# Attention weights turned in half tiles of 64 rows, beside the scores

## The reference

```
for l in range(2):
    h = rms_norm(x, g_pre) @ w_in
    # selected blocks (slc), window 512 (win), compressed keys: 4 heads, head size 64
    # latent attention (mla): 4 heads, query and key size 96, value size 64
    # window 128 (swa): 8 heads, head size 64
    P = softmax(q @ k.T * scale + bias, masked to causal keys)
    o = P @ v
    x = x + rms_norm(concat(o) * silu(z) @ w_out, g_post)
```

## Time and profile before

| | |
|---|---|
| median of 3 runs | 1339.13 us (1339.0 to 1339.31) |
| span of the profiled execution | 1336.9 us |
| attention of layer 0 | about 840 to 975 us of the span |
| attention of layer 1 | about 1145 to 1281 us of the span |
| PE busy | 96% of the span |
| DVE, ACT, POOL busy | 52%, 31%, 30% |

### The profile page before, as it was taken

The page is one execution under the profiler, slowest core; times in us unless marked ns, Lnnn a source line. Parts: engine busy times, 40 slices in busy tenths (PEclk is TensorE's granted clock), DMA queues, the critical chain, the costliest instruction groups (busy, mean ns, idle before and its releaser), DMA issues.

```text
span 1336.9 us, 23888 instructions
## 1 busy us (share of the span) xinstructions
PE 1289.2 (96%) x9603; PEld 792.8 (59%) x9603; DVE 694.1 (52%) x1422; ACT 413.4 (31%) x898; POOL 395.5 (30%) x470
## 2 busy tenths in 40 slices
PE   5999999999999999999999999998999999998997
PEld 3454555655666677678445786445655786445653
DVE  4366667845333344464465373237736383337735
ACT  4243313362432222201014112236613202236721
POOL 0100001221324443153531240128731150127731
PEclk9999999999999999999999999999999999999999
DMA  9710112101410100032244415110003515100001
GB/s 318 267 63 28 37 64 79 63 0 64 142 51 3 65 2 3 2 126 72 94 177 100 129 32 189 64 52 1 2 16 76 147 38 189 63 1 2 1 1 63
DMA packets 71532, 96.54 MB, mean 72 GB/s; under 512 B 27639, under 2 KB 35247, under 8 KB 71422
## 3 DMA queue, kind: packets, MB, share of 16 engines
q1 hardware_dynamic: 71050, 94.76, 21.1%
q10 hardware_dynamic: 372, 0.27, 0.1%
HBM read 92.89 MB, written 2.13 MB: 71 GB/s over the span
## 4 chain that ended last, share of the span: by engine, by line
PE 84%; DVE 5%; SPq 3%; POOL 2%; ACT 2%; issue 1%; DMA 1%; POOLq 0%; DVEq 0%; ACTq 0%
PE PS L147 81%; PE PS L2791 2%; DVE AR L2897 1%; SPq L187 1%; POOL AR L3078 1%; POOL AR L2014 1%; DMA bias_rows<-AR 1%; ACT AR L3019 1%; DMA AR<-in_final_g 1%; SPq L308 1%; SPq L304 0%; SPq L309 0%; SPq L312 0%; POOL AR L3076 0%; DVE AR L2884 0%
## 5 line engine op out<-in xcount | busy, mean ns | idle before, releaser
L147 PE MATMUL PS<-AR 64*64 64x64 f32 (+14 forms) x8966 | 1217.3, 331 | 21.6 <-ACT AR L3029 6.3
L147 PEld LDWEIGHTS PS<-AR 128*128 128x128 f32 (+4 forms) x8966 | 723.4, 155 | 485.6 <-issue 387.0
L3019 ACT ACTIVATE AR<-AR 128x257 f32<-128x257 f32 (+5 forms) x160 | 84.9, 530 | 98.3 <-DVE AR L2897 88.7
L2897 DVE CUSTOM_DVE_ANT_0 AR<-PS,AR 128x257 f32<-128x257 f32 (+5 forms) x160 | 72.3, 452 | 60.7 <-PE PS L147 43.1
L412 POOL TENSOR_TENSOR AR<-AR 128x1 f32<-128x1 f32 (+4 forms) x26 | 21.9, 841 | 258.0 <-DVE AR L407 211.2
L1189 DVE SCALAR_TENSOR_TENSOR AR<-AR 128x441 f32<-128x441 f32 (+2 forms) x96 | 78.6, 819 | 15.7 <-ACT AR L1146 12.0
L1576 DVE TENSOR_TENSOR AR<-PS,AR 128x256 f32<-128x256 f32 x60 | 25.5, 425 | 100.7 <-PE PS L147 97.6
L3078 POOL TENSOR_SCALAR AR<-AR 128x257 f32<-128x257 f32 (+5 forms) x96 | 53.4, 556 | 58.8 <-DVE AR L2903 51.3
L3076 POOL TENSOR_SCALAR AR<-AR 128x128 f32<-128x128 f32 (+3 forms) x64 | 38.9, 608 | 63.3 <-DVE AR L2903 58.3
L1703 ACT ACTIVATE AR<-PS 128x512 f32<-128x512 f32 x48 | 28.7, 597 | 92.5 <-PE PS L147 90.0
L2014 POOL TENSOR_TENSOR AR<-AR 128x512 f32<-128x512 f32 x36 | 47.4, 1318 | 28.0 <-DMA AR<-in_w_o 24.9
(11 more groups left out here) (264 smaller groups left out, 941.6 us busy)
## 6 DMA issues: line engine op xcount, KB each, us to landing
AR<-in_w_in SPq DMA_DIRECT2D x16, 2048.0 KB, 8.9
AR<-in_w_mod SPq DMA_DIRECT2D x6, 2048.0 KB, 12.7
AR<-in_w_out SPq DMA_DIRECT2D x4, 2048.0 KB, 12.5
AR<-in_x SPq DMA_DIRECT2D x8, 512.0 KB, 5.2
AR<-in_w_in SPq DMA_DIRECT2D x4, 1024.0 KB, 7.3
AR<-in_w_o SPq DMA_DIRECT2D x2, 2048.0 KB, 7.7
AR<-in_w_in SPq DMA_DIRECT2D x2, 1664.0 KB, 8.6
AR<-in_w_in SPq DMA_DIRECT2D x12, 256.0 KB, 4.1
```

Source lines behind the costliest of these rows:

```text
L147: return t.matmul(o, l, r, start=s, stop=p, skip_group_check=True)
L2897: v.do.tensor_tensor_reduce(PB[j % NJP][e][:, 0:nk], ps["s", l, j, e][:, 0:nk], bias_for(qb, kind, 2 * a + e, nk), 1.0, 3e38, ALU.add, ALU ...
L3019: a_.do.activation(P, P, ACT.Exp, bias=mn[:, j % NJS, e:e + 1], scale=-1.0, accum_out=su[:, j % NJS, e:e + 1]).then_inc(sa, na("p", l, j, e))
```

## The change

Each 128x128 block of weights is transposed as two half tiles: 64 rows of queries in, 128 rows (keys) by 64 columns out. Rows 0 to 63 go to PSUM bank 3 and rows 64 to 127 to bank 4 of the pair, one after the other. Every job now takes both banks (`take_two`) before its first half tile, and the counter tells that it is turned once, after its last. A narrow job is still one copy, now over both banks; of a wide one DVE copies bank 3 and ACT bank 4, both with both heads' columns. The product reads its 128 columns as two runs of 64. Scores get four banks (0, 1, 2, 5) after the gates. On PE the turn is placed next to the score of its iteration. DVE's and ACT's own sequences stay.

```
-        few = itertools.cycle((0, 1)), itertools.cycle((3, 4))
-        all_ = itertools.cycle((2, 0, 1)), itertools.cycle((5, 3, 4))
+        few, all_ = itertools.cycle((0, 1)), itertools.cycle((0, 1, 2, 5))
...
         def turn(j):
+
             qb, kind, a = JOBS[j]
             k0, nb, nk, at = keys_of(qb, kind)
+            p = ps.take_two(t, "pT", l, j, bank=TURNED)
             for e in range(2):
                 t.wait_ge(sg, ng["normed", l, j, e])
-                if e == 0 or not narrow(j):
-                    p = ps.take(t, "pT", l, j, "both" if narrow(j) else e, bank=next(rings[1]))
-                c = 256 * e if narrow(j) else 0
                 for b in range(nb):
-                    x = t.go.transpose(p[:, c + 128 * b:c + 128 * b + 128], PB[j % NJP][e][:, at[b]:at[b] + 128], ident)
-                if e in halves(j):
-                    x.then_inc(st, nt("pT", l, j, e))
-            if narrow(j):
-                x.then_inc(st, nt("pT", l, j, "both"))
+                    for r in range(2):
+                        c = 512 * r + 64 * (nb * e + b)
+                        x = t.go.transpose(p[:, c:c + 64], PB[j % NJP][e][64 * r:64 * r + 64, at[b]:at[b] + 128],
+                                           ident[64 * r:64 * r + 64, 64 * r:64 * r + 64])
+            x.then_inc(st, nt("pT", l, j))
...
         for i in range(NJ + PV):
-            rings = few if i <= FILLED else all_
-            if i % 2 == 0:
-                turned(i), filled(i), scored(i), summed(i)
+            ring_ = few if i <= FILLED else all_
+            if i <= FILLED and i % 2 == 0:
+                filled(i), turned(i), scored(i), summed(i)
+            elif i <= FILLED:
+                summed(i), scored(i), turned(i), filled(i)
+            elif i % 2 == 0:
+                scored(i), turned(i), summed(i)
             else:
-                summed(i), scored(i), filled(i), turned(i)
+                summed(i), turned(i), scored(i)
...
-        e_.wait_ge(st, nt["pT", l, j, e])
+        e_.wait_ge(st, nt["pT", l, j])
         if j >= NJT:
             e_.wait_ge(st, nt["pv", l, j - NJT])
-        p = ps["pT", l, j, e]
...
         write(dst, src).then_inc(sem, count("pT", l, j, e))
-        ps.empty(sem, count, "pT", l, j, e)
+        ps.empty(sem, count, "pT", l, j)
```

More of the change, by code:

```diff
@@ L2705, in program @@
     TURN, PV = 4, 6
+    TURNED = 3
     CMP_EXP, CMP_SUM, CMP_TURN, CMP_PV = 1, 2, 5, {1: 0, 4: 1}
@@ L2764, in score @@
                 r = slice(64 * e, 64 * e + 64)
-                p = ps.take(t, "s", l, j, e, bank=next(rings[0]))
+                p = ps.take(t, "s", l, j, e, bank=next(ring_))
                 if kind == "mla":
@@ L2776, in score_cmp @@
         def score_cmp(qb):
-            p = ps.take(t, "scc", l, qb, bank=next(rings[0]))
+            p = ps.take(t, "scc", l, qb, bank=next(ring_))
             for a in range(2):
@@ L2784, in turn @@
             k0, nb, nk, at = keys_of(qb, kind)
+            p = ps.take_two(t, "pT", l, j, bank=TURNED)
             for e in range(2):
                 t.wait_ge(sg, ng["normed", l, j, e])
-                if e == 0 or not narrow(j):
-                    p = ps.take(t, "pT", l, j, "both" if narrow(j) else e, bank=next(rings[1]))
-                c = 256 * e if narrow(j) else 0
                 for b in range(nb):
-                    x = t.go.transpose(p[:, c + 128 * b:c + 128 * b + 128], PB[j % NJP][e][:, at[b]:at[b] + 128], ident)
-                if e in halves(j):
-                    x.then_inc(st, nt("pT", l, j, e))
-            if narrow(j):
-                x.then_inc(st, nt("pT", l, j, "both"))
+                    for r in range(2):
[3 more added lines that the diff above has]
+            x.then_inc(st, nt("pT", l, j))
         def turn_cmp(qb):
             t.wait_ge(sg, ng["pc", l, qb])
-            p = ps.take(t, "pcT", l, qb, bank=next(rings[0] if qb else rings[1]))
+            p = ps.take(t, "pcT", l, qb, bank=next(ring_) if qb else TURNED)
             t.go.transpose(p[:, 0:128], Pc.rearrange("p h c -> p (h c)"), ident).then_inc(st, nt("pcT", l, qb))
@@ L2817, in product @@
                         vv = VN_[:, k0 + b, v0:v0 + 64]
-                    x = mm(t.go, o[64 * e:64 * e + 64, c], vv, PT[j % NJT][:, e, 128 * b:128 * b + 128],
-                           b == 0 and kind != "win", b == nb - 1)
+                    x = mm(t.go, o[64 * e:64 * e + 64, c].rearrange("p (r x) -> p r x", r=2), vv,
+                           PT[j % NJT][:, :, 64 * (nb * e + b):64 * (nb * e + b) + 64], b == 0 and kind != "win", b == nb - 1)
             x.then_inc(st, nt("pv", l, j))
@@ L2875, in out_of_psum @@
         w_ = 128 * keys_of(qb, kind)[1]
-        e_.wait_ge(st, nt["pT", l, j, e])
+        e_.wait_ge(st, nt["pT", l, j])
         if j >= NJT:
             e_.wait_ge(st, nt["pv", l, j - NJT])
-        p = ps["pT", l, j, e]
[L2880 to L2883, removed]
+        src, dst = (x[:, :, 0:w_] if e == "both" else x[:, e, 0:w_]
+                    for x in (ps.two("pT", l, j).rearrange("p (r n) -> p r n", r=2), PT[j % NJT]))
         write(dst, src).then_inc(sem, count("pT", l, j, e))
-        ps.empty(sem, count, "pT", l, j, e)
+        ps.empty(sem, count, "pT", l, j)
     def attn_v(v, l):
@@ L2895, in least @@
                 if j >= NJP:
-                    v.wait_ge(st, nt["pT", l, j - NJP, "both" if narrow(j - NJP) else e])
+                    v.wait_ge(st, nt["pT", l, j - NJP])
                 v.do.tensor_tensor_reduce(PB[j % NJP][e][:, 0:nk], ps["s", l, j, e][:, 0:nk], bias_for(qb, kind, 2 * a + e, nk), 1.0, 3e38,
```

## The result

The changed kernel takes 1397.03 us (median of 4 runs, 1394.36 to 1399.03) against 1339.07 us: a ratio of 1.0432, with an interval of 1.0419 to 1.0444. It is slower by 58 us. The forecast was slower, by 16 us, with a range of 1344 to 1371 us; the time lies above it.

What follows compares the result with a forecast made beforehand. PE's order of work bounds the attention's last third, POOL the middle. 6.9 + 1.0 (DVE's lateness) + 1.9 - 1.5 - 0.2 = 8.1 us per layer, 16.2 for two: span 1353.1, median 1355.3 us, range 1344 to 1371.

Steps and rivals of the forecast that it cites:

- The chain: Attention, iterations 13 to 39: score, least, expo, copy, turn stand between two turns; 45.0 us, loop +6.9 per layer; chance 0.78.
- hand-over: Same loop: 13 hand-overs of an estimated 0.05 us behind the waits, 0.6 us per layer.
- Half tiles do overlap: PE's turns: strictly alternating row halves overlap fully, 0.062 us a block, 0.046 less than before.
- The rival of serial halves: PE's turns: half tiles do not overlap, a block costs 0.125 us, 8 us more per layer, 1371 us; chance 0.07.
- the 107 ns each: PE's weight loads: the skill's rule, two loads 213 ns a block, 20 us more in one layer's turns, iterations 13 to 39.
- The rival in which PE gets faster: Attention: both banks are free in time and PE sets the pace, 6.5 us less per layer, 1326 us; chance 0.09.
- the clock stays at 2.4 GHz in the new gaps: PE in the attention: a clock falling in the new gaps would prove the prediction wrong; it fell in no stretch shown.
- The gates' end: From the turns behind the gates to least of 13: 3.3 us in place of 4.8, so -1.5 us per layer.
- the early iterations: Iterations 4 to 11, while the gates run: gate matmuls cover ACT's copy and turns get cheaper, -0.2 us per layer.
- the compressed turns: In the loop of iterations 13 to 39: eight products or turns of compressed keys, 0.45 us each, 3.6 us per layer.
- the sum: From score 13 to score 39: chain, turns, products, compressed keys and hand-overs make 75.6 us per layer, before 68.6.
- The tail: From the score of 39 to the last product: 10.9 us in place of 9.0, so +1.9 us per layer.

Runs made afterwards that it cites:

- e1: Changed kernel with DVE and ACT copying out turned weights ahead of least and expo in every iteration: 1353.2 us, ratio 1.0106.
- e8: Kernel before, with only DVE and ACT copying out turned weights first in every iteration: 1340.5 us, ratio 1.0012.
- e2: Changed kernel with three score banks (0, 1, 2) after the gates in place of four: 1405.6 us, ratio 1.0495.
- e5: e2 plus matmuls whose results nobody reads, sized to each gap ahead of the even turn: 1386.5 us, ratio 1.0351.
- e6: Changed kernel with DVE copying out the turned compressed weights ahead of least in iterations 15, 25 and 35: 1394.4 us, ratio 1.041.
- e7: e1 plus DVE copying out the turned compressed weights ahead of least in iterations 15, 25 and 35: 1346.5 us, ratio 1.0048.
- e4: Kernel before (whole tiles, its own banks) with only PE's new order of steps: 1362.9 us, ratio 1.0176.
- e10: e4 with four score banks, and banks 3 and 4 taken in turn, one by a narrow job: 1362.2 us, ratio 1.018.
- e11: e7 with the compressed weights turned one iteration later, in iterations 6, 16, 26 and 36: 1334.07 us, ratio 0.9968.

## Why the prediction was right in direction and wrong in size

**The chain is what I said it was.** The timeline of iteration 33 after (start, length, instruction):

```profile
967.94 0.46 PE L2792 MATMUL PS<-AR 64*128 64x64 f32 x8
968.18 0.31 PEld L147 LDWEIGHTS PS<-AR 64*128 64x128 f32 x4
969.51 0.69 DVE L2897 CUSTOM_DVE_ANT_0 AR<-PS,AR 128x512 f32<-128x512 f32 x1
971.15 0.72 ACT L3019 ACTIVATE AR<-AR 128x512 f32<-128x512 f32 x1
972.05 0.60 ACT L3029 ACTIVATE AR<-PS 128x512 f32<-128x512 f32 x1
972.71 0.28 PE L2792 MATMUL PS<-AR 64*128 64x64 f32 x2 [2.53 <-ACT AR L3029]
```

The score is loaded at 968.18 and the copy ends at 972.65: 4.47 us, priced at 4.35. The turn of the even iteration follows 0.06 us later, a hand-over priced at 0.05. e1, which takes the copies out of the chain, takes back 44 us; e8 shows that the same edit is worth nothing where no turn waits for the pair of banks.

**Half tiles do overlap.** Eight of them in alternating halves, after:

```profile
914.12 0.46 PE L2792 MATMUL PS<-AR 64*128 64x64 f32 x8
```

Less 0.22 us for the last one, 0.24 us are seven steps: 0.034 us each, against 0.031 predicted. The rival of serial halves falls. So does, for loads that follow each other, the 107 ns each by the rule that the Trainium skill gives (TensorE: Matmul & The Clock Gate, LDWEIGHTS). The rival in which PE gets faster falls by the same waits that carry the chain.

**The step that failed: that the clock stays at 2.4 GHz in the new gaps.** I named its fall as what would make the prediction wrong, and took from the fact that it "did not in any stretch shown here" that it would stay at 1.00. But PE was busy 94 to 96% there, and the chain I had just forecast was to take that away. After, the two loops hold 37.5 and 41.0 us at half clock, and with the rest of the span there are some 98 us (2 x 1395.5 x 0.035), against 8 before. At the 0.29 us for each that e2 and e5 give, the 90 us more are an estimated 26 of the 58 us. The ratio is carried over from two other kernels; the four runs of this one bear it out over 14 us only, and at the 0.53 of e1's layers it would be 48. So it is shown that the clock is a part, and not how large a part.

**The gates' end and the early iterations: +3.2 us in place of -1.7 per layer.** The banks' rule costs there too. In iteration 5 the compressed turn takes bank 3 of the pair behind ACT's copy, which stands behind two exponentials:

```profile
862.02 0.38 ACT L3029 ACTIVATE AR<-PS 128x256 f32<-128x256 f32 x1
...
862.55 0.30 PE L2799 MATMUL PS<-AR 128*128 128x128 f32 x1 [1.81 <-ACT AR L3029]
```

PE is idle for 1.81 us, and the clock is at half for 3.4 us behind it. I had costed the compressed turns as PE's work only. The gain at the gates' end, forecast at 1.5 us, was about 0.4: from the turn behind the gates (897.96) to least of 13 (902.07) it is 4.1 us, with another turn ahead of the gates, in place of 4.8.

**The compressed turns in 15, 25 and 35: no term of the sum had their bank.** They take one of the four score banks, now ahead of the scores of two iterations, and in the second of these the second head's score waits for DVE's copy of them:

```profile
978.67 0.29 DVE L2925 COPY AR<-PS 128x128 f32<-128x128 f32 x1
979.01 2.08 PE L147 MATMUL PS<-AR 96*128 96x512 f32 x2 [1.75 <-DVE AR L2925]
```

From least of 35 to least of 37 the round took 10.25 us (10.9 between the loads of their scores), where the terms of the sum make 6.5. Some of that is clock: from 979 to 985 us, behind this wait, it was 0.50. By itself that wait is nearly covered by the chain (e6: 2.6 us), but it is worth 6.7 us when the chain is gone (e7).

**The tail: +3.7 us in place of +1.9.** The term was there, at half its size; part of it ran at 1.2 GHz (0.87 in the window 993 to 1006).

**The sum.** 16 us as forecast, some 26 for the clock by the estimate above, and some 16 for the early iterations, the compressed turns' banks and the tail, which I get only as the remainder. The range failed with it: its upper end was set by half tiles that don't overlap, and no case in it had the clock, though the text named it. A loss of clock that feeds on a forecast wait should have been one of the rivals, with the chain's own gaps as its condition.

What stays open is the order of PE on its own. I took it as harmless without the pair of banks. e4 and e10 show 23 to 24 us for it, with two different sets of banks, and waits of 9.6 and 2.9 us for ACT's copy in e10. Their mean clocks, 0.987 and 0.993, are some 35 and 19 us at half clock against 8 before. For e10 even 0.53 for each of the 11 us more is 6 of the 23 us, an estimate, so there the waiting is the larger part; no run separates the two.

## What to carry to other kernels

Ahead of making two steps share a buffer, follow who frees it: if the engine that copies it out does so behind work that needs a later step of the producer, a chain closes around the loop, and turning that engine's order round is worth more than the change itself (44 us here, in a kernel where the same reversal had been worth nothing). Whoever forecasts new gaps on TensorE must price what its clock does in them too. And a wait that hides inside a longer one shows its worth only when the longer one is gone (2.6 us, then 6.7 us for the same edit), so try such edits together and in this order.

## What the runs showed of the hardware

The granted clock fell to 1.2 GHz again and again though PE was busy 73 to 82% of the stretches and was never idle for more than 3.1 us at once; in e2, with gaps of 0.5 to 1.7 us ahead of the even turns and of up to 2.1 us ahead of scores, its mean was 0.79 over 98 us. In e11 it stayed at 1.00 in a window of layer 0 in which PE was busy 84% of the time, and was 0.93 from 1200 to 1278 us in layer 1: within one execution the same work kept the clock once and lost it once. Matmuls with no use, put only into the gaps, made a kernel 19.1 us faster (e5 against e2). Half tiles of 64 rows in alternating row halves followed each other at 0.034 us, so two of them, 128x128 in all, took 0.068 us where a whole 128x128 tile took 0.108 us.
